# An even/odd hybrid trunk step: FFN input pieces by order of use, earlier out-projection loads, and FFN groups of 4, 6, 6, 6 in layer 0

## The reference

```
def modulate(x, shift, scale):
    return rms_norm(x) * (1.0 + scale) + shift
def swiglu(h, w_in, w_out):
    g, u = jnp.split(h @ w_in, 2, axis=-1)
    return (jax.nn.silu(g) * u) @ w_out
        xs = xs + ms[2] * os_                       # mixer's out projection, then the FFN:
        xs = xs + ms[5] * swiglu(modulate(xs, ms[3], ms[4]), w_ffn_in[i], w_ffn_out[i])
```

## Time and profile before

| | us |
|---|---|
| runs | 1710.13, 1713.13, 1717.51; median 1713.13 |
| profiled execution | 1715.71, its span 1713.1 |
| TensorE busy | 1623.5 (95%) |
| VectorE busy | 1125.3 (66%) |
| ScalarE busy | 737.5 (43%) |
| mean granted TensorE clock | 0.98 of full |

### The profile page before, as it was taken

One profiled execution on the slowest core, in us unless ns is written; L12 is line 12 of the kernel. 1 busy time (PEld: TensorE's weight loads), 2 busy tenths in 40 slices (PEclk: granted clock), 3 DMA queues, 4 the chain that ended last, 5 costly groups with the idle time before them and its releaser, 6 DMA issues.

```text
span 1713.1 us, 27119 instructions
## 1 busy us (share of the span) xinstructions
PE 1623.5 (95%) x11025; PEld 1497.3 (87%) x11025; DVE 1125.3 (66%) x1892; ACT 737.5 (43%) x1295; POOL 78.3 (5%) x58
## 2 busy tenths in 40 slices
PE   6899996999899999999997999999989999999997
PEld 3589984689899999999997997678989999999997
DVE  5624479576786586585586346854779578588586
ACT  5432563454553243253254444333455335254254
POOL 0000075000000000000000302000000000000000
PEclk9999997999999999999998999999999999999999
DMA  9346223103253553553425113000313313223222
GB/s 318 129 134 215 72 92 103 31 2 99 74 148 105 166 148 107 164 148 118 129 74 166 50 50 101 1 25 1 99 50 93 105 50 89 84 74 91 66 75 90
DMA packets 236837, 168.71 MB, mean 98 GB/s; under 512 B 7925, under 2 KB 232395, under 8 KB 236332
## 3 DMA queue, kind: packets, MB, share of 16 engines
q1 hardware_dynamic: 235796, 166.32, 32.5%
q10 hardware_dynamic: 920, 0.69, 0.2%
HBM read 161.13 MB, written 5.87 MB: 97 GB/s over the span
## 4 chain that ended last, share of the span: by engine, by line
PE 83%; DVE 7%; ACT 3%; SPq 2%; issue 2%; DMA 2%; POOL 1%; ACTq 0%; DVEq 0%
PE ub L1115 6%; PE ub L1117 6%; PE ub L1116 6%; PE ua L1115 6%; PE ua L1117 6%; PE ua L1116 5%; PE ua L1493 5%; PE ub L1493 5%; PE ua L1495 5%; PE ua L1494 5%; PE ub L1495 5%; PE ub L1494 5%; PE pm L1031 2%; PE ua L1347 2%; PE ub L1347 2%
## 5 line engine op out<-in xcount | busy, mean ns | idle before, releaser
L2072 ACT ACTIVATE whi<-weight_sums 128x1024 fp32r<-128x1024 f32 x88 | 93.1, 1058 | 75.0 <-DVE weight_sums L2744 49.5
L1493 PE MATMUL ub<-x_mixed_high,whi 128*128 128x322 f32 x352 | 113.7, 323 | 11.6 <-ACT snap L2135 11.6
L2400 DVE TENSOR_TENSOR wlo<-raw,whi 128x2048 fp32r<-128x2048 f32 (+1 forms) x31 | 58.0, 1872 | 84.6 <-ACT whi L1802 63.3
L1495 PE MATMUL ub<-x_mixed_high,wlo 128*128 128x322 f32 x352 | 111.6, 317 | 0.0
L1494 PE MATMUL ub<-x_mixed_rest,whi 128*128 128x322 f32 x352 | 111.4, 316 | 0.0
L1493 PE MATMUL ua<-x_mixed_high,whi 128*128 128x322 f32 x352 | 110.4, 314 | 0.0
L1495 PE MATMUL ua<-x_mixed_high,wlo 128*128 128x322 f32 x352 | 109.2, 310 | 0.0
L1494 PE MATMUL ua<-x_mixed_rest,whi 128*128 128x322 f32 x352 | 109.0, 310 | 0.0
L2717 DVE TENSOR_TENSOR wlo<-weight_sums,whi 128x1024 fp32r<-128x1024 f32 x88 | 107.2, 1218 | 0.1
L1115 PE MATMUL ub<-hidden_high,whi 128*128 128x384 f32 (+1 forms) x320 | 100.4, 314 | 5.7 <-DVE x L2800 3.7
L1115 PE MATMUL ua<-hidden_high,whi 128*128 128x384 f32 (+1 forms) x320 | 99.9, 312 | 0.9 <-DVE x L2800 0.9
(11 more groups left out here) (675 smaller groups left out, 5114.2 us busy)
## 6 DMA issues: line engine op xcount, KB each, us to landing
raw<-in_w_ffn_in SPq DMA_DIRECT2D x88, 512.0 KB, 5.4
mod_late<-in_w_mod SPq DMA_DIRECT2D x24, 1024.0 KB, 5.3
raw<-in_w_ffn_out SPq DMA_DIRECT2D x48, 384.0 KB, 5.1
modw<-in_w_mod SPq DMA_DIRECT2D x14, 1024.0 KB, 5.3
raw<-in_w_in_even SPq DMA_DIRECT2D x10, 1024.0 KB, 7.8
raw<-in_w_in_odd SPq DMA_DIRECT2D x7, 1024.0 KB, 5.6
mod_first<-in_w_mod SPq DMA_DIRECT2D x5, 1024.0 KB, 12.3
mod_tail<-in_w_mod SPq DMA_DIRECT2D x4, 1024.0 KB, 6.1
```

The lines of the kernel that those rows point to most:

```text
L1493: pe.matmul(dst, wh[:, c], xh, start=first, stop=False, skip_group_check=True)
L1495: ins = pe.matmul(dst, wl[:, c], xh, start=False, stop=last, skip_group_check=True)
L2072: act.activation(ring(whi, g, w), src, ACT.Copy).then_inc(g_hi, 1)
L2400: dve.tensor_tensor(lo, src[s][:, 0:width], hi.bitcast(F32), ALU.subtract).then_inc(w_lo, 1)
```

## The change

- **Pieces.** In `x_tile`, the four mixtures of a high tile are made, copied and subtracted in three steps in the order of their use: `xq[1]`; `xq[0]`, now computed straight from x instead of via a buffer; `xq[2:4]`. `xb`'s rest and `xq[1]`'s rest are counted by a new semaphore, `x_lo`; P2 and P6 of block 0 wait for it tile by tile, and run whole. The mixing buffer shrinks from 4 to 3 pieces.
- **Order within a tile.** ScalarE's `ring_high` moves into `x_tile`, behind the first high piece; its square moves to the end. VectorE's `w_rest` moves behind `x_tile`, and `add_tile` to x_tile's end.
- **Loads.** Out-projection tiles 2 and 3 are issued ahead of block 0's FFN loads.
- **Block 0.** The copy of P1 no longer waits for `h_lo` (VectorE's first combination does); `norm_sum` goes behind P3, and the copy of P6 ahead of `norm_scale`.
- **Groups.** Layer 0 has 4, 6, 6, 6 blocks; layer 1 keeps 6, 6, 6, 4. The tables of modulation loads follow (the same number between products), layer 0's last group keeps tiles 6 and 7 instead of 4 to 7 in `last_w`, and ScalarE's wait in `fast_out_next` is for six output units instead of four.

```diff
-GROUPS = (6, 6, 6, 4)
-NG = len(GROUPS)
+GROUPS = ((4, 6, 6, 6), (6, 6, 6, 4))
+NG = 4
...
-        LATE_IN = {f: NMOD + f - 1 + 2 * (f // 6) for f in range(1, 18)} | {18: 2 * NMOD - 1}
-        LATE_OUT = {(e, m): NMOD + 8 * e + 5 + n for e in range(3) for n, m in enumerate((2, 5))}
+        LATE_IN = ({f: NMOD + f - 1 for f in range(1, 4)} | {f: NMOD + f + 1 for f in range(4, 10)}
+                   | {f: NMOD + f + 3 for f in range(10, 16)} | {f: NMOD + f + 5 for f in range(16, 19)})
+        LATE_OUT = {(e, m): NMOD + 8 * e + 3 + n for e in range(3) for n, m in enumerate((2, 5))}
...
             sp.wait_ge(at_lo, NJ)
+            out_loads(U_OUT0, i_["w_out_even"][0], range(2, 4))
             fast_in_load(0)
-            out_loads(U_OUT0, i_["w_out_even"][0], KD)
+            out_loads(U_OUT0, i_["w_out_even"][0], range(4, KD))
             fast_loads(0)
...
                     if f % NF == 0:
-                        pe.wait_ge(h_lo, KD * Q_FFN[f // NF] + k + (1 if name in ("P1", "P5") else 5))
+                        if name in ("P2", "P6"):
+                            pe.wait_ge(x_lo, KD * (f // NF) + 2 * k + (1 if name == "P2" else 2))
+                        else:
+                            pe.wait_ge(h_lo, KD * Q_FFN[f // NF] + k + (1 if name in ("P1", "P5") else 5))
...
                     product(f, "P5")
-                    product(f, "P2", 0, 3)
+                    product(f, "P2")
                     pe.wait_ge(sn_ok, 4 * f + 1)
-                    product(f, "P6", 0, 3)
-                    product(f, "P2", 3, 4)
-                    product(f, "P6", 3, 4)
-                    norm_sum(Q_FFN[f // NF])
+                    product(f, "P6")
...
                 pe.wait_ge(sn_ok, 4 * f + 2)
                 product(f, "P3")
+                if f % NF == 0:
+                    norm_sum(Q_FFN[f // NF])
...
+                u = U_OUT[layer] + n + 2
+                parts = 12 * layer + (n if n < 4 else 2 * n - 4)
+                if n >= 1:
+                    act.wait_ge(h_lo, KD * q + n)
+                if n >= 4:
+                    for v, (a, c) in enumerate(((LH, LS), (LS, T))):
+                        ins = act.activation(xmix[:, 1, 2 + a - LH:2 + c - LH], x[:, k, a:c], ACT.Copy, scale=b.negscale[:, k, v:v + 1])
+                    ins.then_inc(hmod, 1)
                 act.wait_ge(x_up, KD * (NG + 1) * layer + n + 1)
-                act.wait_ge(xm_s, KD * layer + n)
-                if n >= 5:
-                    act.wait_ge(h_lo, KD * q + n)
-                act.activation(xmix[:, 0, 2:2 + LS - LH], x[:, n, LH:LS], ACT.Copy, scale=s0)
-                act.activation(xmix[:, 0, 2 + LS - LH:HW], x[:, n, LS:T], ACT.Copy, scale=s1).then_inc(hmod, 1)
+                if n < 4:
+                    act.activation(xmix[:, 0, 2:2 + LS - LH], x[:, n, LH:LS], ACT.Copy, scale=s0)
+                    act.activation(xmix[:, 0, 2 + LS - LH:HW], x[:, n, LS:T], ACT.Copy, scale=s1).then_inc(hmod, 1)
                 high = b.xa_hi[:, k, 0] if n < 4 else b.xb_hi[k][:, :]
                 act.activation(high[:, 0:2], shift, ACT.Copy)
                 act.activation(high[:, 2:HW], x[:, n, 0:LH], ACT.Copy, scale=s0).then_inc(h_hi, 1)
-                act.wait_ge(ssq_added, KD * q + n - 1)
-                act.activation(sq[:, n % 2], x[:, n], ACT.Square, scale=D ** -0.5).then_inc(sq_ready, 1)
-                act.wait_ge(xm_s, KD * layer + n + 1)
+                if n < 6:
+                    ring_high(u, 1024)
+                act.wait_ge(xm_s, parts + 1)
                 if n < 4:
                     act.activation(b.xa_hi[:, k, 1, 0:2], shift, ACT.Copy, scale=0.0)
                     act.activation(b.xa_hi[:, k, 1, 2:HW], xmix[:, 1, 2:HW], ACT.Copy).then_inc(h_hi, 1)
                 else:
-                    act.activation(b.xq_hi[k][:, :, :], xmix[:, :, :], ACT.Copy).then_inc(h_hi, 1)
+                    high = b.xq_hi[k]
+                    act.activation(high[:, 1], xmix[:, 0], ACT.Copy).then_inc(h_hi, 1)
+                    act.activation(high[:, 0, 0:2], shift, ACT.Copy)
+                    act.activation(high[:, 0, 2:2 + LS - LH], x[:, n, LH:LS], ACT.Copy, scale=s0)
+                    act.activation(high[:, 0, 2 + LS - LH:HW], x[:, n, LS:T], ACT.Copy, scale=s1).then_inc(h_hi, 1)
+                    act.wait_ge(xm_s, parts + 2)
+                    act.activation(high[:, 2:4], xmix[:, 1:3], ACT.Copy).then_inc(h_hi, 1)
+                act.wait_ge(ssq_added, KD * q + n - 1)
+                act.activation(sq[:, n % 2], x[:, n], ACT.Square, scale=D ** -0.5).then_inc(sq_ready, 1)
 
...
-                if n == 0 and f % NF == 0:
-                    act.wait_ge(h_lo, KD * Q_FFN[f // NF] + KD)
-                elif n == 0:
+                if n == 0 and f % NF:
                     act.wait_ge(f_add, 4 * f - 2)
...
                     snapped(f, 1)
+                    snapped(f, 2)
                     norm_scale(Q_FFN[f // NF])
...
                 if n < 4:
+                    dve.wait_ge(h_hi, high + 2)
                     dve.tensor_tensor(b.xa_lo[:, k, 1, 2:HW], xmix[:, 1, 2:HW], b.xa_hi[:, k, 1, 2:HW].bitcast(F32),
                                       ALU.subtract).then_inc(h_lo, 1)
                 else:
-                    dve.tensor_tensor(b.xq_lo[k][:, :, :], xmix[:, :, :], b.xq_hi[k][:, :, :].bitcast(F32), ALU.subtract
-                                      ).then_inc(h_lo, 1)
+                    ins.then_inc(x_lo, 1)
+                    hi, lo = b.xq_hi[k], b.xq_lo[k]
+                    dve.wait_ge(xm_s, parts + 1)
+                    dve.scalar_tensor_tensor(xmix[:, 2, 2:HW], x_, neg[:, n, 0:1], xmix[:, 0, 2:HW],
+                                             ALU.mult, ALU.add).then_inc(xm_s, 1)
+                    dve.wait_ge(h_hi, high + 2)
+                    dve.tensor_tensor(lo[:, 1], xmix[:, 0], hi[:, 1].bitcast(F32), ALU.subtract).then_inc(x_lo, 1)
+                    dve.wait_ge(h_hi, high + 3)
+                    dve.tensor_tensor(lo[:, 0, 0:2], shift, hi[:, 0, 0:2].bitcast(F32), ALU.subtract)
+                    dve.scalar_tensor_tensor(lo[:, 0, 2:e], x[:, n, LH:LS], scale(n), hi[:, 0, 2:e].bitcast(F32),
+                                             ALU.mult, ALU.subtract)
+                    dve.scalar_tensor_tensor(lo[:, 0, e:HW], x[:, n, LS:T], scale(n, 1), hi[:, 0, e:HW].bitcast(F32),
+                                             ALU.mult, ALU.subtract)
+                    dve.wait_ge(h_hi, high + 4)
+                    dve.tensor_tensor(lo[:, 2:4], xmix[:, 1:3], hi[:, 2:4].bitcast(F32), ALU.subtract).then_inc(h_lo, 1)
+                add_tile(q, n)
 
...
                     dve.sem_inc(x_up, 1)
-                    if n == 0:
-                        x_shifts(layer)
+                    x_tile(layer, n)
                     if n < 6:
                         w_rest(u + 2, u % 2, 1024)
-                    x_tile(layer, n)
```

More of the change, by code:

```diff
@@ L358, in build_program @@
         ta = area(hh_at, sb_at["ident"])
-        first.hid_hi, first.hid_lo = (ta(f"hidden_{n}_0", [P, GROUPS[0], T], F32R) for n in ("high", "rest"))
+        first.hid_hi, first.hid_lo = (ta(f"hidden_{n}_0", [P, max(GROUPS[0]), T], F32R) for n in ("high", "rest"))
         mod_late = ta("mod_late", [P, 2048])
-        first.last_w = sb("last_weights_0", [P, 4, 2, GROUPS[-1] * P], F32R, at=sb_at["modw0"])
+        first.last_w = sb("last_weights_0", [P, 2, 2, GROUPS[0][-1] * P], F32R, at=sb_at["modw0"])
         ta = area(hh_at, sb_at["ident"])
@@ L369, in build_program @@
         ta = area(phase_at, b_end)
-        second.hid_hi, second.hid_lo = (ta(f"hidden_{n}_1", [P, GROUPS[0], T], F32R) for n in ("high", "rest"))
+        second.hid_hi, second.hid_lo = (ta(f"hidden_{n}_1", [P, max(GROUPS[1]), T], F32R) for n in ("high", "rest"))
         second.xq_lo.append(ta("x_mixed3_rest_1", [P, 4, HW], F32R))
@@ L547, in build_program @@
         xm_s = sem("x_parts_combined")
+        x_lo = sem("x_pieces_rest_ready")
         fin_c = sem("result_gained")
@@ L566, in build_program @@
         count = [0, 0, 0, 0]
-        for gn in 2 * GROUPS:
+        for gn in GROUPS[0] + GROUPS[1]:
             for f in range(gn):
@@ L578, in build_program @@
             count = [count[0] + KD, count[1] + KD, count[2] + KD, count[3] + KD]
-        FIRST_F = [sum((2 * GROUPS)[:e]) for e in range(2 * NG)]
-        GROUP = 2 * GROUPS
+        GROUP = GROUPS[0] + GROUPS[1]
+        FIRST_F = [sum(GROUP[:e]) for e in range(2 * NG)]
+        LAST_RING = (6, 4)
         G_LAYER, Q_LAYER, IN_U_LAYER = (0, in_g[NF]), (0, in_q[NF]), (0, in_u[NF])
@@ L606, in out_place @@
         def out_place(e, m, n):
-            if e % NG == NG - 1 and m >= 4:
-                return fast[e // NG].last_w[:, m - 4, n]
+            layer = e // NG
+            if e % NG == NG - 1 and m >= LAST_RING[layer]:
+                return fast[layer].last_w[:, m - LAST_RING[layer], n]
```

(23 more changed lines are left out.)

44 lines of the change are left out of this document (19 added, 25 removed).

## The result

The changed kernel takes 1702.38 us (median of 8 runs, 1699.23 to 1706.92) where the kernel before took 1710.33 beside it (8 runs, 1707.51 to 1717.51): 0.9947 of the time, with an interval of 0.9931 to 0.9964. Its profiled execution took 1701.01 us, 14.7 less than the one of before; how that fits a median only 8 lower is told further down.

What follows compares the result with a forecast made beforehand. TensorE was taken as the bound (83% of the span), so only its waits and half-clock time could be won. Input stages 9.2 plus regrouping 6.2 made 15.4 us off 1715.7: 1700.3, median forecast 1698, range 1687 to 1708.

Steps and rivals of the forecast that it cites:

- The forecast case: Whole kernel: long waits replaced by smaller ones plus regrouping gain, 1698 us, chance 0.56.
- Out weights first: Out-projection unit 2: earlier tile 2 load cuts its wait from 2.55 to 0.3 us.
- Pieces in order of use: Out-projection units 3 to 7: VectorE waits for ScalarE in each tile, 3.8 us of new waits per layer.
- Own counts and first copy: FFN block 0's sixth product, P6: waits 0.4 us where it waited 3.24.
- Sixth copy ahead of the row scale: Blocks 0 and 1: P7's 2.58 us wait goes; block 1's P1 waits 1.9, its P3 1.5 more (2.3 in layer 1).
- 4, 6, 6, 6: Layer 0's FFN groups: 9.6 us won, less 2.6 at group 0's unit 5 and 0.8 for clock: 6.2 net.
- The clock: Input stage of each layer: 4.8 us lost at half clock before; one stretch of 1.6 us charged after.
- The sum: Whole kernel: 9.2 + 6.2 = 15.4 us off the profiled 1715.7 gives 1700.3; median 2.6 lower, so 1698.
- A: Rival, input stage: VectorE bounds it, three half-clock stretches stay, 1.4 us gained per layer; 1704 to 1706 us, chance 0.16.
- B: Rival, layer 0's groups: regrouping leaves only 1 of 6.2 us; 1703 us, chance 0.10.
- C: Rival, input stages: small waits before units 2 to 7 keep TensorE at 1.2 GHz; 1740, or half, 1719 us; chance 0.05.
- D: Rival, whole kernel: no half-clock stretch, few VectorE waits, group 0 hidden, 28 us gained; 1685 us, chance 0.13.

Runs made afterwards that it cites:

- the second time: The changed kernel itself, unaltered, run once more beside the kernel before on one chip: 1702.45 us, 0.9921 of the kernel before.
- the third experiment: The changed kernel with ScalarE's copy and VectorE's subtraction of the out weights put back ahead of the pieces in each tile: 1693.85 us, 0.9897 of the kernel before.

## Why the prediction was right

The forecast case held in its mechanism: the three long waits go, smaller ones come between, and the regrouping gives six. The time lay in the range, but in size it was less of a hit: 15.1 us were forecast off the median of the runs shown, and 8.0 were measured, with an interval of 6.2 to 11.8 (12.2 the second time, 9.8 to 17.1 by its ratio).

- *Out weights first.* Unit 2's 2.55 us went: no wait in layer 0, 1.05 in layer 1 (0.3 forecast). But this step was worth more than I laid on it. I kept 3.8 us of VectorE waits and one half-clock stretch against it, and so never saw that by itself it is worth 5.8 to 6.0 per layer in those traces: block 0 comes 4.3 earlier (+49.84 for +54.14), which is the 2.55 us wait and the 1.6 of the stretch behind it. The rest falls in blocks 0 and 1 (35.11 us for 36.59); their waits are the same 3.24 and 2.57, and there is one half-clock stretch less behind them, which this edit doesn't explain.
- *Pieces in order of use.* The mechanism was right, VectorE idle for ScalarE in each tile (0.94 and 0.78 ahead of the two rows above; 0.83 and 0.88 forecast), and the weights-first run shows that it is the cause. Units 2 to 7 were forecast to wait 4.1 us in sum; in layer 1 they wait 1.05, 1.39, 0.30, 0.29, 1.04 and nothing, 4.07, in layer 0 2.33 and 0.94. That the sum agrees is in part luck, as loads are in it: unit 2's 1.05 stands behind ScalarE waiting 1.02 for the load of tile 2, and 0.8 of unit 3's 1.39 goes with the FFN load. With tile 3 behind the FFN loads, units 3 to 7 wait 2.21 in layer 1, and I had 3.8. The starts show some 0.2 us more for each (1199.52 to 1208.25 is 8.73, where 7.12 + 1.39 make 8.51), and so block 0 starts at +55.39 and +55.20, some 1.2 later than forecast.
- *The term that was missed.* Of the 2.33 ahead of unit 3 in layer 0 (I had 0.8), 1.8 is not a handover. Tiles 2 and 3 now stand ahead of the FFN loads, so these are issued at 393.52 instead of 391.44, and the sums of the FFN weights stand in VectorE's program ahead of unit 3's subtraction. VectorE waits 1.70, in the second execution 2.90. I had moved the loads and priced only the one that came earlier. The wait bites only in this order: with the weights first, VectorE waits 2.17 for the same load, and no unit waits. Of the one half-clock stretch per layer, layer 0 had two, the first behind this wait, and layer 1 none; in the other two traces of this order layer 0 had one of twice the length, and layer 1 one and none.
- *Own counts and first copy.* 0.4 forecast, 0.33 measured. The late units hid the rest: with the units on time P6 waits 1.57.
- *Sixth copy ahead of the row scale.* P7's wait went. Block 1's P1 waits 1.74 and 1.75 (1.9), and its P3 waits 1.99 in layer 1 (2.3). In layer 0 it doesn't wait (1.5 forecast). The second stretch at 0.51 there, 466.2 to 469.6, gives ScalarE time; with the stretch gone, in the weights-first run, P3 waits 1.03 there.
- *4, 6, 6, 6.* 6.2 forecast; 5.9 in the whole change, 6.1 alone. Unit 5 of group 0 waits 1.77 (2.6, upper end 3.5); the last tile waits 1.14 and 3.09 (about 4). Unforecast: the two ends of this term could be removed, 6.0 and 2.0 us, since the second weight pair and the modulation load need not stand where they did.
- *The clock.* I had laid 3.2 of the 4.6 us per layer on it (three stretches of 1.6 before, one after) and only 1.4 on waits and small things. That was the right place: in layer 1 the waits fell by 0.3 us and the clock gave the rest. But it is also the term that moves most from one execution to the next. In the changed kernel's two traces layer 1 stays at 1.00 through eight waits of 0.28 to 1.99 us; in everything but the regrouping, with the same order there, one stretch at half clock follows a wait of 1.76. The Trainium skill's clause on swings from frequent small idles (page "TensorE: Matmul & The Clock Gate", section "A second HAM failure mode: psum-queue depth-cycling") would, by my reading, have made these stages slower than before; at these sizes no stage here shows such swings.
- *The sum.* Per layer 4.0 and 4.5 for 4.6, and 5.9 for 6.2: 14.4 for 15.4, and the profiled execution came at 1701.01 where the sum said 1700.3. The term that failed in size is the last one, from that execution to the median. I took it for 2.6 above the median of three runs; over eight runs it is 5.4 above, while the profiled execution after lies 1.4 below its own. 14.7 - 5.4 - 1.4 = 7.9, the gain that was measured. A sum made on one execution carries that execution's clock: 26 runs of the kernel before spread from 1707.62 us at a mean granted clock of 0.983 to 1719.12 at 0.977; a straight line through all of them has 1.4 us for each 0.001. The stages carry it too. The mean over the traces with each stage code is 89.9 and 88.9 us before (two traces) and 87.8 and 86.2 after (three), a gain of 2.2 and 2.7 per stage where the table has 4.0 and 4.5; with the 5.9 that is 10.7, between the 8.0 and the 12.2 of the medians.

Of the rivals, A had the mechanism but not the price, as its half-clock stretches didn't outlast the long waits in layer 1. The time doesn't speak against it: its gain of 9.0 us (1.4 per layer and 6.2) is nearer to the measured 8.0 than the forecast's 15.4. What does is the clock in the stages, with one or two stretches in layer 0 and none or one in layer 1 where A had three. B was wrong on the regrouping, which gave 5.9 and not 1, and near the measured time by accident. C is excluded by the window at 1.00. D's 1685 shows what was there to take: with the weights ahead of the pieces, the norm's sum put back, block 1's weight copy ahead of the row scale, and the pair and the load moved, it is 1679.71.

## What to carry to other kernels

Where two engines hand pieces to and fro, keep an independent piece of work between the handovers; to sort a program by which product needs what first takes that cover away, and it cost 4.1 us in the stage where both kernels ran at full clock. When a load is moved up, price those that it is moved ahead of, and find the instruction that waits for each in its engine's order. Place a gain by landmarks in two traces, ask of each stage how much of it is waits and how much is clock, and trust it no further than a second trace of the same code agrees.

## What the hardware showed that I hadn't expected

Some executions of the same program spend a whole stretch of the start, 31 to 68 us, at a granted clock of 0.50, others at 0.91; unit 1 then starts 9.5 us later (402.97 for 393.45). The regrouping-alone kernel, the same up to there, also had 0.50 and unit 1 at 402.96; two others had 0.68 and 0.69, with unit 1 at 399.85 and 398.75. What decides it is open: no kernel here was made to change it.

The fall behind a wait isn't a matter of its length alone. Long waits can leave the clock alone: with the loads alone, P7's wait of 2.57 in layer 0 (461.56, shown above) lies in a window at 1.00, and with the groups alone P6's wait of 3.24 in layer 0 was followed by 7.8 us at 1.00.

```profile
457.50:478.87 21.37, 18.80 (x135) 17.77 (x134) 15.96 (x25) 13.99 (x21) 0.00 (x0) 1.00 0.46 133
```
```profile
465.40:473.20 7.80, 5.27 (x31) 4.69 (x31) 1.99 (x4) 6.24 (x10) 0.00 (x0) 1.00 0.45 128
```

Short ones can be followed by a fall. In the changed kernel's layer 1, waits of 1.75 and 1.99 us in 10 us left the clock at 1.00; in its layer 0 a wait of 1.74 was followed by 3.4 us at 0.51, 54 us after another such stretch. In the third experiment the same 1.74 in layer 0 left the stage at 1.00; what decides it is open:

```profile
460.94 0.42 PE L1496 MATMUL ua<-x_first_high,whi 128*128 128x322 f32 x1 [1.74 <-DVE wlo L2730]
```
```profile
393.70:476.00 82.30, 77.95 (x527) 76.00 (x526) 69.12 (x143) 50.61 (x102) 0.00 (x0) 1.00 0.39 114
```
